# A layer with sparse attention on one core: sample compression in eighths, sample stages with loads and small operations reordered, merge started by depth

## The chip, the cores and the metric

One NeuronCore of a Trainium2 chip runs the whole program. The metric is device time in microseconds for one execution, lower is better. The profiled execution and the timed runs are different executions of the same program.

## The reference

One layer is applied to a prompt of 1024 tokens (model width 1024) and to 8 sample rows, each with 2048 past rows in paged caches. Three branches are computed: native sparse attention (attention over compressed keys, over selected blocks, and over a window, mixed by gates), a chunkwise mLSTM, and attention over a memory. Then the branches are merged and a feed-forward follows. The parts that the change touches:

```python
past_cmp = cache_kv_cmp[page_table].reshape(...)
rows_s = jnp.concatenate([past_cmp, kv_cmp_s], axis=1)
k_c, v_c, end_c = compress_kv(rows_s, cmp_pe, cmp_w1, cmp_b1, cmp_w2, k_norm_cmp)   # 127 blocks per sample
o_cmp_s, p_cmp_s = dense_attend(q_s, k_c, v_c, end_c[None, :] <= pos_s[:, None])
idx_s, valid_s = select_blocks(p_cmp_s, pos_s, -(-rows_s.shape[1] // SLC_BLOCK))     # the ranking
sel_s = gather_blocks_paged(cache_kv_slc, page_table, kv_slc_s, idx_s)
o_slc_s = slc_attend(q_rot_s, sel_s, idx_s, valid_s, pos_s)
o_win_s, win_s = win_sample(q_rot_s, kv_win_s, cache_kv_win, pos_s)
o_mem_s = mem_attend(mq_raw, cache_kv_mem, mem_q_norm)
...
yb = jnp.einsum('bsnc,ncd->bsnd', jnp.stack([o_nsa, o_ml, o_mem], axis=2), w_branch)
g = jax.nn.sigmoid(gate_raw.reshape(B, S, N_BRANCH, D_MODEL))
x = x + (g * yb).sum(2) @ w_out
```

## The kernel before

The kernel is written with explicit semaphores: each engine has its own instruction list in each block, and a block ends with a barrier of all engines, so the last engine of a block sets when the next one starts. Between the groups of stages the semaphores are cleared as well (`Stage.renew`). The stages run in this order: norm, mLSTM projections, mLSTM, sample compression (`stage_s_compress`), attention of the prompt (`stage_attention`: token projections, memory, turning, compression, and `stage_slc_win`), samples (`stage_samples`), and the tail (merge, output projection, feed-forward).

Matmuls are made exact in three passes: an operand is split into a high part (`high`, ScalarE, L160) and a low part (`low`, VectorE, L165), and `products` issues three matmuls for each pair (L177, L178, L179).

**Sample compression.** For each batch b of 8, the pages are in SBUF in a double buffer. A fill (`fill`, L2557) is 8 transposes into two PSUM banks; there are four fills for a batch, in two bank pairs in turn. Each fill is split by ScalarE (4 activations, L160) and then VectorE (4 subtractions, L165). Fill f waits until fill f-2 has been split (`x_low >= f - 1`). A batch's 96 matmuls come in four quarters of 24; a fill of the next batch stands before each quarter. The first quarter of a batch waits until all four fills of that batch are split. `project` (L2585) applies the second weight to the activated result of the batch before. At the end SyncE stores the compressed keys and values to DRAM (`kc_kept`, `vc_kept`), loads a weight of the next stage (L2536), and waits for three stores before the block's end (L2517). The second store of keys has its own semaphore `spilled`, for which ScalarE waits near the start of the token projections (L1434).

**Samples.** `stage_s_prep` loads the page table and the kept keys and values, turns the small sample rows, and waits for the loads. `stage_s_select` scores the compressed keys, takes the softmax, multiplies by the values, ranks the blocks by a 33 by 33 comparison and spreads the result; meanwhile SyncE and GpSimd issue the first loads of the next block. `stage_s_attend` goes through 24 units: window, memory and selected blocks for each batch (the last batch has the memory last). For unit u TensorE does `turn(u+1)`, `scores(u)`, `attend(u-2)`, `turn_p(u-1)`; ScalarE keeps half of the turned keys, does `softmax(u)` (L3063) and then `keep_p(u-1)` (L3074 for memory, L3076 and L3077 otherwise); VectorE keeps the other half, does `gather(u)` and `use(u-2)` (L3154, L3146). `attend(u-2)` on TensorE waits for `keep_p(u-2)` and for `use(u-3)`.

**Merge.** 72 steps of 36 matmuls: a weight tile l of 24 by a third of the tokens b. Before step 0, the first weight tile and the tokens have to be split. The first piece is four of the eight depth slices k.

## Time and profile before

| | before |
|---|---|
| median of 3 runs | 2583.96 us (2579.82 to 2584.76) |
| the profiled execution's own time | 2569.68 us |
| span of its trace | 2568.1 us |
| TensorE busy | 2389.3 us, 93% |
| VectorE busy | 1216.1 us, 47% |
| ScalarE busy | 813.6 us, 32% |
| mean granted TensorE clock | 0.965 of full speed |

The rows below are read so: a group of instructions is named by its line in the kernel, its engine and its operation, with output and input tiles. In a timeline, the first number is the start in microseconds from the span's start, the second the time until the end of the last instruction merged into the row, and the brackets hold the idle time of the engine before it and who ended it. PEclk is the granted TensorE clock as a share of 2.4 GHz, so 0.50 is 1.2 GHz.

### The profile page before, as it was taken

The numbers are of one execution on the slowest core, as the hardware profiler recorded it, in microseconds if no ns is written. First come the engines' busy times: TensorE is split into PE (matmuls) and PEld (weight loads), VectorE is DVE, ScalarE is ACT, GpSimd is POOL, SyncE is SP. The second block draws the span as 40 slices with busy tenths as digits, with TensorE's granted clock in tenths as the row PEclk, the third lists the DMA queues.
The fourth block names the chain that finished last, engine by engine and source line by source line (L and its number), as shares of the span: only waits on it lengthen the run. The fifth ranks groups of instructions, "written<-read, shape, count | busy, mean of one in ns | idle before, by whom it ended". The sixth has DMA issues, their size and how long they took to land. (4 is left out here: it accounts for less than half of the span.)

```text
span 2568.1 us, 40403 instructions
## 1 busy us (share of the span) xinstructions
PE 2389.3 (93%) x15386; PEld 2177.1 (85%) x15386; DVE 1216.1 (47%) x2160; ACT 813.6 (32%) x1779; POOL 321.0 (13%) x570
## 2 busy tenths in 40 slices
PE   6988897999877999878799999999999999999999
PEld 6977787999766889744499999987999999999997
DVE  4457665313757777466532323334434333333334
ACT  5354454444435665323321112221311111111110
POOL 1014221012204322355100000000000000000000
PEclk9998699999999999889899999999999999999999
DMA  5012432321110000277301112130211111111111
GB/s 154 21 34 67 137 109 80 98 99 34 43 35 1 1 1 1 56 183 179 98 25 50 50 42 78 50 116 1 83 50 49 34 50 50 50 39 44 50 33 66
DMA packets 216412, 156.77 MB, mean 61 GB/s; under 512 B 76338, under 2 KB 197349, under 8 KB 216164
## 3 DMA queue, kind: packets, MB, share of 16 engines
q1 hardware_dynamic: 186708, 121.96, 16.8%
q0 software_dynamic: 8160, 19.08, 2.8%
q10 hardware_dynamic: 21360, 13.22, 1.7%
q8 instruction: 123, 2.02, 0.3%
q14 instruction: 61, 0.50, 0.1%
HBM read 142.76 MB, written 15.59 MB: 62 GB/s over the span
## 5 line engine op out<-in xcount | busy, mean ns | idle before, releaser
L177 PE MATMUL ps<-brT_r,ff_wih 128*128 128x344 f32 x1008 | 322.0, 319 | 0.0
L179 PE MATMUL ps<-brT_r,ff_wi_r 128*128 128x344 f32 x1008 | 321.6, 319 | 0.0
L178 PE MATMUL ps<-xnT_r,ff_wih 128*128 128x344 f32 x1008 | 321.3, 319 | 0.0
L3765 ACT ACTIVATE ff_sa<-ps 128x344 f32<-128x344 f32 x66 | 30.3, 459 | 563.5 <-PE ps L179 563.5
L177 PE MATMUL ps<-x_r,mg_wh 128*128 128x344 f32 x576 | 185.4, 322 | 6.5 <-DVE xnT_r L165 6.5
L177 PEld LDWEIGHTS ps<-brT_r,ff_wih 128*128 128x128 f32 x1008 | 189.6, 188 | 1.0
L179 PEld LDWEIGHTS ps<-brT_r,ff_wi_r 128*128 128x128 f32 x1008 | 189.4, 188 | 0.0
L178 PEld LDWEIGHTS ps<-xnT_r,ff_wih 128*128 128x128 f32 x1008 | 189.0, 187 | 0.4
L178 PE MATMUL ps<-xnT_r,mg_wh 128*128 128x344 f32 x576 | 184.7, 321 | 0.0
L3801 DVE TENSOR_TENSOR x<-x,ps 128x512 f32<-128x512 f32 (+1 forms) x198 | 134.8, 685 | 100.9 <-PE ps L179 100.2
L179 PE MATMUL ps<-x_r,mg_w_r 128*128 128x344 f32 x552 | 176.2, 319 | 0.0
L2001 PE MATMUL ps<-a_kvsw,att_pT 128*128 128x128 f32 x1056 | 142.5, 279 | 14.9 <-ACT brT L2047 6.4
L177 PE MATMUL ps<-x_r,brT_r 128*128 128x256 f32 (+3 forms) x504 | 143.4, 285 | 7.2 <-DVE xnT_r L165 7.2
L2001 PEld LDWEIGHTS ps<-a_kvsw,att_pT 128*128 128x128 f32 x1056 | 129.2, 193 | 19.5 <-ACT att_pT L1947 11.6
L178 PE MATMUL ps<-x_r,brT_r 128*128 128x256 f32 (+3 forms) x504 | 143.0, 284 | 0.0
L179 PE MATMUL ps<-x_r,xnT_r 128*128 128x256 f32 (+3 forms) x504 | 142.8, 283 | 0.0
L3344 ACT ACTIVATE mg_sg<-ps 128x344 f32<-128x344 f32 x72 | 33.0, 458 | 319.9 <-PE ps L179 319.9
L177 PEld LDWEIGHTS ps<-x_r,mg_wh 128*128 128x128 f32 x576 | 109.3, 190 | 6.6 <-issue 6.6
L165 DVE TENSOR_TENSOR sc_xl<-ps,brT_r 64x512 fp32r<-64x512 f32 x128 | 88.2, 689 | 47.0 <-ACT brT_r L160 45.6
L178 PEld LDWEIGHTS ps<-xnT_r,mg_wh 128*128 128x128 f32 x576 | 109.1, 189 | 0.0
L2062 ACT ACTIVATE att_p<-ps,att_mx 128x640 f32<-128x640 f32 (+7 forms) x128 | 89.6, 700 | 55.7 <-DVE att_mx L2090 54.5
L3391 DVE TENSOR_TENSOR mg_tm<-mg_sg,ps 128x344 f32<-128x344 f32 x48 | 24.6, 512 | 172.0 <-ACT mg_sg L3344 172.0
(618 smaller groups left out, 5871.5 us busy)
## 6 DMA issues: line engine op xcount, KB each, us to landing
ff_wi<-in_w_ffn_in SPq DMA_DIRECT2D x42, 512.0 KB, 5.2
mg_w<-in_w_in SPq DMA_DIRECT2D x23, 512.0 KB, 4.2
ff_wo<-in_w_ffn_out SPq DMA_DIRECT2D x11, 1024.0 KB, 4.9
s_pages<-in_cache_kv_slc POOLq DMA_DIRECT2D x128, 64.0 KB, 2.8
s_pages<-in_cache_kv_slc SPq DMA_DIRECT2D x128, 64.0 KB, 2.8
sc_X<-in_cache_kv_cmp SPq DMA_DIRECT2D x56, 128.0 KB
sc_X<-in_cache_kv_cmp POOLq DMA_DIRECT2D x56, 128.0 KB, 2.4
mg_w<-in_w_branch SPq DMA_DIRECT2D x23, 256.0 KB, 4.6
```

The source lines that it names most:

```text
L165: return nc.vector.tensor_tensor(lo, x, hi.bitcast(F32), ALU.subtract)
L177: nc.tensor.matmul(out, wh, xh, start=(first and k == 0), stop=False)
L178: nc.tensor.matmul(out, wh, xl, start=False, stop=False)
L179: ins = nc.tensor.matmul(out, wl, xh, start=False, stop=(last and k == n - 1))
L2001: ins = nc.tensor.matmul(ps[:, 6 + u % 2, 0:P], pT[:, u % 2, b * P:(b + 1) * P], kv, start=(b == 0), stop=(b == hi - lo - 1))
L2062: nc.scalar.activation(p_[:, u % 2, 0:n], src, ACT.Exp, scale=-1.0, bias=mx[:, u % 4:u % 4 + 1], accum_out=sm[:, u % 4:u % 4 + 1]).then_in ...
L3344: nc.scalar.activation(sg[:, s % 2, :], ps[:, s % 4, 0:BLK], ACT.Sigmoid).then_inc(gated, 1)
L3391: chain.link(dve, nc.vector.tensor_tensor(tm, sg[:, s % 2, :], ps[:, 4 + s % 4, 0:BLK], ALU.mult))
L3765: nc.scalar.activation(sa[:, s % 2, :], ps[:, s % 2, 0:BLK], ACT.Silu).then_inc(silued, 1)
L3801: nc.vector.tensor_tensor(dst, dst, ps[0:m, 4 + i % 4, :], ALU.add).then_inc(added, 1)
```

## The change

Six places are edited:

1. Sample compression: a batch's products are issued in eighths of 12 matmuls in place of quarters of 24. The four fills stand before eighths 0, 1, 3 and 4; `project` stands after eighth 3. ScalarE's first activation of the batch and VectorE's `out` stand after the fourth split in place of the third. SyncE's last store of values is moved ahead of the weight load.
2. The kept keys and values are loaded in `stage_slc_win`, after the last query has been turned, into a part of `x2`; `stage_s_prep` no longer loads or waits for them. The page table's wait goes to SyncE and GpSimd in front of the page loads of `stage_s_select`.
3. In `stage_s_select` the multiplication by the gate (L2834) is moved behind the ranking.
4. In `stage_s_attend` ScalarE's `keep_p(u-1)` is moved ahead of `softmax(u)`.
5. At the end of `stage_s_attend` eight copies become four of twice the size.
6. Merge: the first weight tile is split in pieces of depth (0:1), (1:4), (4:12), and the first third of the tokens in (0:1), (1:2), (2:3), (3:4), (4:8); step 0 waits for each slice by itself.

```diff
@@ stage_slc_win
+        last_q = max(m for m, x in enumerate(items) if x[0] == "q")
+            @block.sync
+            def _(sp):
+                sp.wait_ge(pturned, last_q + 1)
+                for dst, name in zip(kept_rows(M), ("kc_kept", "vc_kept")):
+                    sp.dma_start(dst, M[name]).then_inc(M["kept_in"], 16)
+def kept_rows(M):
+    flat = M["x2"][:, :, :].rearrange("p t d -> p (t d)")
+    return flat[0:HD, 0:B * G * NCS], flat[:, 2048:2048 + B * G * HD]
@@ stage_s_prep
-                sp.dma_start(A["pt"][:, :], I["page_table"].rearrange("b n -> (b n)").unsqueeze(0)).then_inc(loaded, 16)
-                sp.dma_start(A["kcT"].rearrange("p n q -> p (n q)"), M["kc_kept"]).then_inc(loaded, 16)
-                sp.dma_start(A["vc"][:, :, :, :].rearrange("p b g d -> p (b g d)"), M["vc_kept"]).then_inc(loaded, 16)
-                sp.wait_ge(loaded, 48)
+                sp.dma_start(A["pt"][:, :], I["page_table"].rearrange("b n -> (b n)").unsqueeze(0)).then_inc(A["pt_in"], 16)
@@ stage_s_compress, SyncE
-                sp.wait_ge(hid, 2 * B)
-                sp.dma_start(tok_weights(M, 1, "raw"), tok_group(M, 1)).then_inc(M["tok_in1"], 16)
                 sp.wait_ge(okept, B)
                 sp.dma_start(M["vc_kept"][:, VE:], vc[:, :, :, :].rearrange("p b g d -> p (b g d)")[:, VE:]
                              ).then_inc(stored, 16)
+                sp.wait_ge(hid, 2 * B)
+                sp.dma_start(tok_weights(M, 1, "raw"), tok_group(M, 1)).then_inc(M["tok_in1"], 16)
@@ stage_s_compress, TensorE
                 for b in range(B):
-                    for k in range(4):
-                        if b + 1 < B:
-                            fill((b + 1) * NF + k)
-                        quarter(b, k)
-                        if k == 1 and b >= 1:
+                    for e in range(8):
+                        if b + 1 < B and e in (0, 1, 3, 4):
+                            fill((b + 1) * NF + (0, 1, 3, 4).index(e))
+                        eighth(b, e // 2, e % 2)
+                        if e == 3 and b >= 1:
                             project(b - 1)
@@ stage_s_compress, ScalarE and VectorE
-                        if k == 2:
+                        if k == 3:
                             gelu(b, 0)
-                        if k == 2 and b >= 1:
+                        if k == 3 and b >= 1:
                             out(b - 1)
@@ stage_s_select
+                sp.wait_ge(A["pt_in"], 16)
                 load_kinds(sp, M["I"]["cache_kv_slc"], A["pages"], A["pt"], 0, 0, A["in_k"][0], A["in_v"][0])
...
+                pe.wait_ge(M["kept_in"], 32)
...
-                dve.wait_ge(attended, 1)
-                nc.vector.tensor_tensor(oacc[:, :, :], ps[0:H, 4:6, :]..., bc(gT[:, 0, :], 2, P), ALU.mult)
                 dve.wait_ge(attended, 2)
...
                 nc.vector.tensor_scalar(imp[:, :], cnt[:, :], 15.5, -BIG, ALU.is_ge, ALU.mult).then_inc(ranked, 1)
+                nc.vector.tensor_tensor(oacc[:, :, :], ps[0:H, 4:6, :]..., bc(gT[:, 0, :], 2, P), ALU.mult)
                 dve.wait_ge(spread, 1)
@@ stage_s_attend, ScalarE
-                    softmax(u)
                     if u >= 1:
                         keep_p(u - 1)
+                    softmax(u)
@@ stage_s_attend, VectorE
-                for h in range(H):
-                    lo, g = (h % 2) * HD, h // HPG
-                    nc.vector.tensor_copy(brT[lo:lo + HD, h // 2, S:T], src)
+                for g in range(G):
+                    for q in range(2):
+                        nc.vector.tensor_copy(brT[q * HD:(q + 1) * HD, 2 * g:2 * g + 2, S:T], rows[:, 2 * g:2 * g + 2, q, :])
@@ stage_merge
+    W_FIRST = ((0, 1), (1, 4), (4, 12))
+    X_FIRST = ((0, 1), (1, 2), (2, 3), (3, 4), (4, 8))
+                    if s == 0:
+                        for k in range(4):
+                            pe.wait_ge(w_low, 1 if k == 0 else 2)
+                            pe.wait_ge(x_low, k + 1)
+                            products(nc, ps[:, 0, 0:BLK], terms[k:k + 1], first=(k == 0), last=False)
```

## Rows read from the trace of the kernel before

**Rows 1.** Tail stretch: PE, PEld, DVE, ACT, POOL busy, clock, DMA share, GB/s.
```profile
1289.00:2568.00 1279.00, 1271.63 (x7357) 1189.86 (x7355) 467.74 (x628) 229.12 (x321) 5.57 (x11) 1.00 0.17 51
```

**Rows 2.** Waits, 280 to 440 us: total, times, longest.
```profile
PE ps L177 <- DVE sc_xl L165: 11.9, 7, 2.4
```

**Rows 3.** Timeline, sample compression, 395 to 421 us: start, duration, what, idle before.
```profile
396.42 1.03 PE L2557 MATMUL ps<-cst,sc_X 128*128 128x128 f32 x8
...
397.21 0.36 PE L177 MATMUL ps<-brT_r,x_r 128*128 128x256 f32 x1
...
397.49 2.41 ACT L160 ACTIVATE brT_r<-ps 64x512 fp32r<-64x512 f32 x4 [0.78 <-PE ps L2557]
...
399.93 2.79 DVE L165 TENSOR_TENSOR sc_xl<-ps,brT_r 64x512 fp32r<-64x512 f32 x4 [0.37 <-ACT brT_r L160]
...
400.20 1.04 PE L2557 MATMUL ps<-cst,sc_X 128*128 128x128 f32 x8
...
420.54 0.38 PE L177 MATMUL ps<-brT_r,x_r 128*128 128x256 f32 x1 [2.39 <-DVE sc_xl L165]
```

**Rows 4.** Timeline, end of compression and start of the next stage.
```profile
442.51 0.50 SPq L2541 DMA_DIRECT2D kc_kept<-brT  x1
...
447.01 7.22 ACT L160 ACTIVATE brT_r<-xnT 128x512 fp32r<-128x512 f32 x7 [10.68 <-PEq L102]
```

**Rows 5.** DMA issues, 430 to 447 us: count, KB, us to landing.
```profile
kc_kept<-brT SPq DMA_DIRECT2D x1, 127.0 KB, 3.5
```

**Rows 6.** SyncE's waits over the whole span: total, times, longest.
```profile
SPq L2380 <- DMA s_vc<-vc_kept: 4.7, 1, 4.7
...
SPq L2517 <- DMA vc_kept<-sc_vc: 2.6, 1, 2.6
```

**Rows 7.** Timeline, sample preparation and selection.
```profile
1071.19 0.16 DVE L2419 COPY s_gT<-ps 8x24 f32<-8x24 f32 x1
...
1075.54 5.02 SPq L2771 DMA_DIRECT2D s_vrow<-memT  x8
...
1088.83 1.21 DVE L2834 TENSOR_TENSOR s_oacc<-ps,s_gT 8x1024 f32<-8x1024 f32 x1 [3.14 <-PE ps L2801]
...
1098.17 0.42 DVE L2851 COPY s_selneg<-ps 8x264 f32<-8x264 f32 x1 [1.14 <-PE ps L2809]
...
1101.00 0.94 PE L3032 MATMUL ps<-s_knT,s_qz 128*8 128x1 f32 x32 [2.87 <-PEq L2764]
```

**Rows 8.** SyncE's 16 page issues in the selection: first and last start.
```profile
L2440 SPq DMA_DIRECT2D s_pages<-in_cache_kv_slc x16: 542/543/1119, 1088.1 to 1099.8; - x16
```

**Rows 9.** Waits, 1101 to 1277 us.
```profile
PE ps L3021 <- ACT sa_pT L3074: 14.1, 7, 2.1
```

**Rows 10.** Timeline, sample attention: one batch, and two later starts of L3021.
```profile
1138.46 2.00 ACT L3063 ACTIVATE sa_s<-sa_s,sa_mx 8x2049 f32<-8x2049 f32 x1 [6.44 <-DVE sa_mx L3131]
...
1138.71 0.34 DVE L3154 SCALAR_TENSOR_TENSOR s_oacc<-ps,sa_sm,s_oacc 8x128 f32<-8x128 f32 x1
...
1140.66 1.88 PE L3021 MATMUL ps<-x,sa_pT 128*4 128x512 f32 x4 [2.13 <-ACT sa_pT L3074]
...
1223.58 2.43 PE L3021 MATMUL ps<-x,sa_pT 128*4 128x512 f32 x4 [2.14 <-ACT sa_pT L3074]
...
1247.40 1.02 PE L3021 MATMUL ps<-s_rows,sa_pT 128*4 128x512 f32 x2 [1.26 <-ACT sa_pT L3074]
```

**Rows 11.** Two short stretches, columns as in rows 1.
```profile
1226.00:1228.00 2.00, 2.00 (x19) 1.96 (x19) 1.77 (x2) 0.12 (x1) 1.56 (x3) 0.50 0.68 144
...
1286.00:1288.00 2.00, 2.00 (x14) 2.00 (x13) 2.00 (x3) 2.00 (x3) 0.00 (x0) 0.95 0.00 0
```

**Rows 12.** Timeline, end of the sample attention and first matmul of the merge.
```profile
1274.14 1.41 DVE L3178 COPY brT<-ps 64x8 f32<-64x8 f32 x8 [1.84 <-PE ps L3051]
...
1278.90 1.59 DVE L165 TENSOR_TENSOR xnT_r<-xnT,x_r 128x1376 fp32r<-128x1376 f32 x1 [0.55 <-ACT x_r L160]
...
1280.64 0.62 PE L177 MATMUL ps<-x_r,mg_wh 128*128 128x344 f32 x1 [6.54 <-DVE xnT_r L165]
```

More of the change, by code:

```diff
@@ L2377, in stage_s_prep @@
         sem = st.sem
-        turned, kept, loaded = (sem(n) for n in ("turned", "kept", "loaded"))
+        turned, kept = (sem(n) for n in ("turned", "kept"))
         chain = Chain(sem("step"))
@@ L2559, in fill, with eighth @@
                     ins.then_inc(turned, 1)
-                def quarter(b, k):
-                    cc = k // 2
-                    if k == 0:
+                def eighth(b, k, part_):
+                    cc, lo = k // 2, k % 2 * 8 + 4 * part_
+                    if k == 0 and part_ == 0:
                         pe.wait_ge(x_low, NF * (b + 1))
-                    if k % 2 == 0 and b >= 1:
+                    if lo == 0 and b >= 1:
                         pe.wait_ge(activated, 2 * (b - 1) + cc + 1)
-                    if k % 2 == 0 and b == 0:
+                    if lo == 0 and b == 0:
                         pe.wait_ge(w_low, cc + 1)
@@ L2572, in quarter @@
                                    [((w1h[:, cc, r, :], w1l[:, cc, r, :]), (part(xh, r), part(xl, r)))
-                                    for r in range(k % 2 * 8, k % 2 * 8 + 8)], first=(k % 2 == 0), last=(k % 2 == 1))
-                    if k % 2:
+                                    for r in range(lo, lo + 4)], first=(lo == 0), last=(lo == 12))
+                    if lo == 12:
                         ins.then_inc(hid, 1)
@@ L3194, in stage_samples @@
         A["rows0"] = st.sb("rows", [P, 2, 2048])[:, :, :]
+        A["pt_in"] = st.sem("pt_in")
         for n in ("in_win", "in_mem"):
@@ L3294, in _ @@
                     n, j = loads[l]
-                    if b == 0:
-                        pe.wait_ge(w_low, l + 2 if l else 1)
-                    if l == 0:
-                        pe.wait_ge(x_low, 2 * b + 1)
+                    if b == 0 and l:
+                        pe.wait_ge(w_low, l + 3)
+                    if l == 0 and b:
+                        pe.wait_ge(x_low, x_count(b) + 1)
                     if s >= 4:
@@ L3330, in _ @@
                 act.wait_ge(M["mg_in"][0], 16)
[L3331 removed]
+                split_first(slice(*W_FIRST[0]))
                 for b in range(NB3):
[L3333 to L3335 removed]
+                    for lo_, hi_ in x_pieces(b):
+                        high(nc, xh[:, lo_:hi_, tok(b)], xnT[:, lo_:hi_, tok(b)]).then_inc(x_high, 1)
+                        if b == 0 and lo_ == 0:
+                            split_first(slice(*W_FIRST[1]))
+                        if b == 0 and lo_ == 3:
                             act.wait_ge(M["mg_in"][1], 16)
[L3337 removed]
+                            split_first(slice(*W_FIRST[2]))
                     split_b(0, b)
```

46 lines of the change are left out of this document (24 added, 22 removed).

## The prediction

> **What bounds the kernel now.** I read the stretches by stage first, then TensorE's waits in each, then the timeline around each wait, then SyncE's own waits. From 1289 us to the end TensorE is busy 1271.63 of 1279 us at full clock [rows 1]: the feed-forward and most of the merge hold nothing to win, and whatever is saved ahead of them moves them as a block. Ahead of them TensorE is the engine that sets the pace inside the stages, and stage boundaries are set by whoever arrives last. The reader should see four places where TensorE or a boundary waits: seven waits of 11.9 us in all in the sample compression [rows 2], two DMA waits of SyncE at block ends, 2.6 and 4.7 us [rows 6], seven waits of 14.1 us in the sample attention [rows 9], and the 6.5 us before the merge's first matmul [rows 12].
>
> **Compression in eighths.** A fill takes TensorE 397.21 - 396.42 = 0.79 us; a fill and a quarter take 400.20 - 396.42 = 3.78, so an eighth is (3.78 - 0.79) / 2 = 1.5. ScalarE begins 1.07 after the fill's start and takes 2.41, VectorE follows with 2.79: a fill is split some 6.3 us after it began [rows 3]. Between the last fill of a batch and the next batch's first quarter TensorE has only 0.79 + 3.0 + 0.79 of work, so it waits: 2.39 in the last case, where no fill stands between [rows 3], and (11.9 - 2.39) / 6 = 1.58 in the six others [rows 2]. After the change, from a batch's start at 0: fill 0 ends at 0.8, eighth 0 at 2.3, fill 1 at 3.1, eighths 1 and 2 at 6.1. Fill 2 needs fill 0 split, at 6.3 to 6.4: a new wait of about 0.25. It ends at 7.15, eighth 3 at 8.65, `project` at 9.5. Fill 3 needs fill 1 split. ScalarE took fill 1 behind the first activation, at 4.0, so VectorE ends it at 9.2: no wait. Fill 3 begins at 9.5, its ScalarE part at 10.6, its VectorE part at 13.05 and ends at 15.85, and the four eighths run to 16.35. The next batch's first eighth then finds its data ready, also in the last batch. The old waits go (11.9), seven new ones of 0.25 and 0.03 of slack in each come (2.0): a gain of 9.9 us. Bounds: 11.9 if the new wait is nothing; 6 if each of the seven is 0.8, that is, if the splits behind the closer pair of fills end half a microsecond late. ScalarE's activation moved behind the fourth split is wanted only by the next batch's first eighth, 2.8 us later. The page loads wait for fills that now come earlier, so they are not late.
>
> **The store moved ahead of the weight load.** SyncE waits 2.6 us for the small store of values at the stage's end [rows 6]. Moved ahead, it lands before SyncE gets there, and the block can end 2.6 earlier. But something is late next: the next stage's ScalarE first waits for the last store of keys (`spilled`), issued at 442.51 and landing after 3.5, at 446.0 [rows 4, 5]; ScalarE's first instruction there starts at 447.01 [rows 4]. That store is not moved. So only 447.0 - 446.05 = 0.95 is gained. SyncE's weight load is one issue later and is wanted much later. Bounds 0.3 (the load now sits directly ahead of the keys in the queue) and 2.6.
>
> **Kept keys and values loaded in the attention.** SyncE is idle there and nothing is queued behind its wait for the last query. In the preparation SyncE waits 4.7 [rows 6] while VectorE ends at 1071.35 and the next block starts at 1075.54 [rows 7]. Without the two loads VectorE is last; with the 0.45 us that a block's end took after SyncE's wait, the next block starts at 1071.8: gain 3.75. The page table is waited for later, behind 8 + 4 + 1 issues on SyncE and the 2.4 us of GpSimd's mask, 2.5 us or more after its issue at 1068.9. Bounds 3.2 and 4.2.
>
> **The gate behind the ranking.** VectorE's chain loses 1.21 us at 1088.83 [rows 7] and gets the operation back under TensorE's spreading, where VectorE waits 1.14 anyway [rows 7]. But VectorE ends at 1098.59, and TensorE's next block starts at 1101.00 [rows 7]. Who is last is SyncE: its sixteenth page issue starts at 1099.8 and takes 0.54 [rows 8], ending at 1100.3. That queue is neither shortened nor moved against the block's start. So I cost this at 0. Bounds -0.1 and 1.1.
>
> **Probabilities kept first.** The memory unit's `keep_p` stands behind the 2.00 us softmax of the selected blocks on ScalarE, though its input is ready: TensorE is through at 1138.53 and attends at 1140.66, after 2.13 idle [rows 10]. Ahead of the softmax, `keep_p` is done near 1136.6. Then `attend` waits for VectorE's `use` of the window unit, which ends at 1138.71 + 0.34 = 1139.05 [rows 10]. This is the late thing next: TensorE starts at 1139.1 and not 1138.5, keeping 0.6 of idle in six batches, so 14.1 - 3.6 = 10.5 is gained. The softmax of the selected blocks isn't delayed, as `keep_p` is over by then. The other pairs: the window's softmax now waits for the turned probabilities of the selected unit, some 1 us later than now, and the memory's for those of the window unit, 3 us later; both are wanted by TensorE over 4 us after that. Bounds 3 (the softmax's end, 1140.55 [rows 10], governs the following turn, and everything else with it) and 12.5.
>
> **The clock.** In the sixth of these batches the granted clock is 0.50 (1.2 GHz) at 1226 to 1228 us [rows 11], right after one such idle time. From 1140.66 to 1223.58 four batches take 20.73 each; the next interval is 23.82 [rows 10], so 3.1 us more. With idle times a third as long I expect no such fall: gain 3.1, bounds 0 and 3.1.
>
> **Copies at the end.** Eight copies take 1.41 [rows 12], 0.18 each; four of twice the elements (16 for 64 partitions) at 0.18 give 0.7: gain 0.7, bounds 0.3 and 0.9.
>
> **Merge by depth.** VectorE's subtraction on four slices takes 1.59 and ends at 1280.49, 3.5 us after the block's start; TensorE follows at 1280.64 [rows 12]. By depth the first piece is a quarter: TensorE can start about 1.3 after the block's start, 2.35 earlier. It then does a slice each 0.86 at the half clock and ends the fourth at 4.9. The second half of the tokens is split no earlier than now (6.2 after the start, since VectorE's total is the same), so TensorE pauses 1.3. The clock rose near 1286.1, so 5.4 us after the first matmul [rows 11, 12]; if it rises as long after the new start, the rest runs at the full clock, and step 0 ends at 10.1 in place of 11.9 after the block's start. I take 1.3. Bounds 1.9, and -1.1 if the pause puts the rise off by its own start over again. TensorE, from 1289 us on, never waits, so this passes to the end.
>
> [...]
>
> **The sum.** 9.9 + 0.95 + 3.75 + 0 + 10.5 + 3.1 + 0.7 + 1.3 = 30.2 us. The profiled execution took 2569.68, which becomes 2539.5. The median of the timed runs is 14.3 higher; I take the same gain from it: 2583.96 - 30.2 = 2553.8, say 2554.
>
> **Rivals.** (a) The fills collide: closer fills wait for VectorE each time and the compression gains 4 instead of 9.9, time 2560. For it: two of four fills now follow an eighth after another. Against: VectorE and ScalarE both have idle time in each batch [rows 3]. Chance 0.10. (b) Another wait takes the place in the attention: `turn_p` waits for the softmax or `attend` for `use`, and with the clock term it gains 4 instead of 13.6, time 2563.5. For it: VectorE's 1139.05 and ScalarE's 1140.55 [rows 10] stand close ahead of the old times. Against: TensorE's own 1.88 of `attend` fills that stretch. Chance 0.12. [...] Chance 0.2, inside the range. (d) Slower: in the sample attention, 176 us long, the granted clock stays at 1.2 GHz. By the timeline the half clock lasted some 7 us and cost 3.1, so 0.45 a microsecond; the gain of 27.1 outside the clock term is gone when it lasts over 60 us, and the kernel is slower by 0.2% from 72. At 90 us the time is 2583.96 - 27.1 + 40.5 = 2597. Against: idle times get shorter. Chance 0.03. (e) The moved loads don't do what they should, because the preparation is held by something else as long: time 2557.5. Chance 0.05, inside the range too.
>
> **The numbers.** My forecast 0.7 (with (c) and (e) as variants of it), (a) 0.10, (b) 0.12, (a) and (b) together 0.03, (d) 0.03, rest 0.02. The lower end takes the good bounds of compression, store and attention (2, 1.6, 2) and a little for the runs' scatter: 2545. The upper one takes in (a) and (b) singly: 2566. Under 0.2%, 5.2 us, a measurement of this kernel can hardly tell from no change; faster by more than that 0.95, the same 0.02, slower 0.03.
>
> **What would show it.** Compression: no wait before L177 in batches 1 to 7, small waits of 0.25 before L2557; intervals between batches of 16.3 in place of 17.7. Boundary: no DMA wait at SyncE's L2517, and ScalarE's first instruction about 1 us earlier against the last key store. Preparation: the block after it 0.45 us behind VectorE's last copy. Selection: 25.4 us long as before, SyncE last. Attention: waits of TensorE for L3074 gone, about 0.6 for L3154 in their place, interval 19.2 in place of 20.7, clock 1.00. Merge: first matmul 1.3 after the block's start, a pause of 1.3 in step 0. It is wrong if new waits before L2557 sum to over 6 us, if intervals in the attention stay above 20, or if the clock drops where it didn't before.

## The result, and the profile after

Four timed executions of the kernel before, the three of the table ahead of the prediction among them, have a median of 2581.89 us (2577.26 to 2584.76); four of the changed kernel have 2543.01 (2541.01 to 2544.89). The ratio is 0.9856, 95% interval 0.9835 to 0.9877: 38.9 us, 1.5%, faster. The forecast was 2554 us with a range from 2545 to 2566: the sign is right, the gain was larger than forecast, and the time lies 2.0 us below the range. The profiled execution took 2543.22 (span 2541.6), 26.5 less than the profiled one of before (2569.68), and that is less than the 30.2 that I summed. So the steps have to be read one by one, and two questions stay for the runs: which terms were wrong, and why the timed gain is 12 us more than that between the two profiles.

The stage's waits in the compression (290 to 440 us; total, times, longest), to be held against [rows 2]:

```profile
PE ps L2569 <- DMA sc_X<-in_cache_kv_cmp: 3.8, 1, 3.8
PE ps L2569 <- DVE sc_xl L165: 2.3, 7, 1.1
```

The wait of L177 for `sc_xl` is gone, and the fills (L2569) wait instead. Of the seven waits in the last row, the longest (1.05 us, at 289.76) stands in the kernel before as well, ahead of the first batch; the new ones are six of 0.17 to 0.23 us, 1.2 us in all, where the prediction counted seven of 0.28. The timeline of one batch shows one of them, in the middle of the batch:

```profile
329.82 1.04 PE L2569 MATMUL ps<-cst,sc_X 128*128 128x128 f32 x8
...
332.13 1.04 PE L2569 MATMUL ps<-cst,sc_X 128*128 128x128 f32 x8
...
336.24 1.09 PE L2569 MATMUL ps<-cst,sc_X 128*128 128x128 f32 x8 [0.17 <-DVE sc_xl L165]
...
346.19 1.03 PE L2569 MATMUL ps<-cst,sc_X 128*128 128x128 f32 x8
```

A batch is 346.19 - 329.82 = 16.37 us long; forecast 16.35. Now the end of the stage, and the preparation with the selection, which answer to [rows 4, 7]:

```profile
433.28 0.51 SPq L2553 DMA_DIRECT2D kc_kept<-brT  x1
...
437.18 3.38 ACT L160 ACTIVATE brT_r<-xnT 128x512 fp32r<-128x512 f32 x3 [10.09 <-DMA kc_kept<-brT]
...
1063.18 0.16 DVE L2431 COPY s_gT<-ps 8x24 f32<-8x24 f32 x1
...
1063.82 5.04 SPq L2785 DMA_DIRECT2D s_vrow<-memT  x8
...
1084.63 1.20 DVE L2863 TENSOR_TENSOR s_oacc<-ps,s_gT 8x1024 f32<-8x1024 f32 x1
1085.84 0.42 DVE L2867 COPY s_selneg<-ps 8x264 f32<-8x264 f32 x1
...
1089.49 0.94 PE L3048 MATMUL ps<-s_knT,s_qz 128*8 128x1 f32 x32 [3.69 <-PEq L2778]
```

ScalarE's first instruction behind the compression names the last store of keys as what released it, as forecast; the block itself started at 435.73, so the values' store no longer holds it. From the issue of that store to ScalarE's first instruction it is 3.90 us in place of 4.50, which is 0.6 gained where 0.95 was forecast: the store took 3.9 us to land and not 3.5. The block behind the preparation starts 0.48 us behind VectorE's last copy (1063.34 to 1063.82): the 4.7 us of [rows 6] are gone. In the selection VectorE is done at 1086.26 and the next block begins at 1089.45. SyncE's page issues there (count, then duration in ns, then first and last start) end last, at 1088.2 + 0.54, as in [rows 8]:

```profile
L2452 SPq DMA_DIRECT2D s_pages<-in_cache_kv_slc x16: 542/543/1337, 1076.4 to 1088.2; - x16
```

The sample attention and the merge stand against [rows 9, 10, 11, 12]: first the waits from 1105 to 1252 us, then the timeline, then two stretches with the granted clock in the third column from the end.

```profile
PE ps L3037 <- DVE s_oacc L3171: 4.4, 7, 0.7
...
PE ps L3037 <- ACT sa_pT L3093: 0.5, 1, 0.5
```

```profile
1108.17 1.88 PE L3037 MATMUL ps<-s_rows,sa_pT 128*4 128x512 f32 x4 [0.67 <-DVE s_oacc L3171]
...
1127.43 1.02 PE L3037 MATMUL ps<-x,sa_pT 128*4 128x512 f32 x2 [0.67 <-DVE s_oacc L3171]
...
1249.95 0.73 DVE L3195 COPY brT<-ps 64x16 f32<-64x16 f32 x4 [1.25 <-PE ps L3067]
...
1253.49 0.62 PE L177 MATMUL ps<-x_r,mg_wh 128*128 128x344 f32 x1 [3.58 <-DVE xnT_r L165]
...
1258.21 0.43 PE L177 MATMUL ps<-x_r,mg_wh 128*128 128x344 f32 x1 [1.06 <-DVE xnT_r L165]
```

```profile
1110.00:1250.00 140.00, 133.20 (x880) 73.25 (x879) 90.09 (x188) 43.55 (x103) 67.26 (x94) 1.00 0.67 162
...
1262.00:2541.00 1279.00, 1272.55 (x7358) 1190.88 (x7356) 469.98 (x629) 231.53 (x323) 5.57 (x11) 1.00 0.17 51
```

The forecast signs are there: waits of 0.67 us for `use` in place of 2.13 for `keep_p`, batches 19.26 us apart (forecast 19.2), the clock 1.00 from 1110 to 1250 us, four copies in 0.73, TensorE's first matmul 1.42 us behind the merge block's start (1252.07), a pause of 1.06, and from there to the end a TensorE as busy as in [rows 1]. The waits moved as forecast. What was wrong is the size of terms and the time that they were taken from, and it took repeats of the kernel before to see which.

### The profile page after: what moved, and what is told of

Read it like the earlier page. It is cut to its first block and busy times, and to the rows that moved or that the text cites. A ratio compares the mean times of both kernels' runs of the same rounds, so it can differ in the third digit from the quotient of the medians.

```text
span 2541.6 us, 40409 instructions
## 1 busy us (share of the span) xinstructions
PE 2392.3 (94%) x15386; PEld 2180.1 (86%) x15386; DVE 1216.2 (48%) x2160; ACT 813.7 (32%) x1783; POOL 321.1 (13%) x570
## 5 line engine op out<-in xcount | busy, mean ns | idle before, releaser
L177 PE MATMUL ps<-brT_r,ff_wih 128*128 128x344 f32 x1008 | 322.0, 319 | 0.0
L177 PEld LDWEIGHTS ps<-brT_r,ff_wih 128*128 128x128 f32 x1008 | 189.6, 188 | 1.0
L177 PE MATMUL ps<-x_r,mg_wh 128*128 128x344 f32 x576 | 185.1, 321 | 4.6 <-DVE xnT_r L165 4.6
L177 PE MATMUL ps<-x_r,brT_r 128*128 128x256 f32 (+3 forms) x504 | 143.6, 285 | 6.6 <-DVE xnT_r L165 6.6
L177 PEld LDWEIGHTS ps<-x_r,mg_wh 128*128 128x128 f32 x576 | 108.8, 189 | 5.1 <-DVE memT_r L165 3.6
```

The costliest lines, as they stand in the source:

```text
L177: nc.tensor.matmul(out, wh, xh, start=(first and k == 0), stop=False)
```

## The experiments

Each kernel was timed beside the kernel before on the same chip; the comparisons below ran on four chips, on which the kernel before has medians of 2575.4 to 2577.8 us. "By part" below means the length of a stretch between the same two matmuls of two traces. A "fall" is a stretch in which the granted clock is 0.50 between stretches at 1.00; a "full" one costs 3.08 us, a "short" one 1.6.

**The kernel before, again.** No edit.

> The kernel before, unchanged, profiled and timed once more. Its three timed executions took 2579.8 to 2584.8 us, its profiled one 2569.7, while the changed kernel's profiled execution (2543.2) lies among its timed ones (2541.0 to 2544.9). Theory 1: the profiled execution of before was an untypically quick one; this one should take 2578 to 2585, and its timeline of granted clocks should show where the 12 us lie: more half-clock stretches right behind waits in the sample attention (up to six falls of some 3 us each in place of one) or in the sample compression. Theory 2: profiled executions of this kernel are simply quicker than timed ones: again 2570 profiled beside 2580 timed, with the same single fall of the clock. Ratio to the kernel before 1.000 within 0.002 in both.

Twelve executions have a median of 2577.64 us (2570.20 to 2581.57), and the twenty-four that they were compared with 2576.8 (2566.5 to 2583.3); the profiled one took 2578.6. The trace shows the fall of the clock behind TensorE's wait for `keep_p` not once but twice (first stretches, with the clock in the third column from the end; then the matmuls behind the waits):

```profile
1211.00:1216.00 5.00, 5.00 (x33) 4.85 (x33) 2.46 (x3) 1.24 (x4) 3.27 (x5) 0.50 0.81 201
1235.00:1240.00 5.00, 5.00 (x33) 4.90 (x33) 2.93 (x4) 1.04 (x3) 2.88 (x4) 0.50 0.84 218
```

```profile
1188.01 1.88 PE L3021 MATMUL ps<-x,sa_pT 128*4 128x512 f32 x4 [2.14 <-ACT sa_pT L3074]
...
1208.74 2.43 PE L3021 MATMUL ps<-s_rows,sa_pT 128*4 128x512 f32 x4 [2.14 <-ACT sa_pT L3074]
...
1232.56 2.35 PE L3021 MATMUL ps<-x,sa_pT 128*4 128x512 f32 x4 [2.14 <-ACT sa_pT L3074]
```

The waits are as long as ever, 2.14. From 1188.01 to 1208.74 it is 20.73, from 1208.74 to 1232.56 it is 23.82: the half clock costs 3.08 us, and it can be told by the matmuls' own 2.43 in place of 1.88. A shorter stretch at 0.50, behind the first of the waits (1124.20), costs 1.6 more. Theory 1 holds in kind (more falls), with two and not six. Of the 9.0 us between the two profiles of the same kernel these are 4.7; the rest is scatter elsewhere, by part 2.4 before the compression, 0.4 at its end, 0.5 in the attention of the prompt and 1.2 ahead of the first wait of the sample attention. Over the executions the time goes with the mean granted clock: 0.967 at 2567.3 us, 0.959 at 2583.3.

**Probabilities kept first, alone.**

```diff
-                    softmax(u)
                     if u >= 1:
                         keep_p(u - 1)
+                    softmax(u)
```

> The kernel before with one edit: in the sample attention ScalarE keeps the probabilities of the previous unit ahead of the softmax. The prediction gave this 10.5 us of waits and 3.1 of clock, 13.6 in all. Theory 1 (the timed executions of before lose a further 12 us in falls of the clock behind these very waits): 22 to 27 us faster in the timed medians, and the granted clock is 1.00 over the stage. Rival (the further 12 us lie in a part that this edit doesn't touch): 10.5 to 14 us faster. Other rival (no effect beyond the moved wait): under 5.

2560.19 us against 2576.8: ratio 0.9941 (0.9928 to 0.9954), 16.6 us. That is between the two expectations, 10.5 to 14 and 22 to 27. The waits and the clock over the stage:

```profile
PE ps L3021 <- DVE s_oacc L3155: 4.4, 7, 0.7
```

```profile
1120.00:1260.00 140.00, 134.48 (x869) 72.50 (x867) 91.24 (x194) 46.01 (x105) 68.91 (x96) 1.00 0.67 165
```

The waits are those of the changed kernel, and there is no fall. By part, the waits give 10.2 us; the falls give 3.08 against the trace that stands ahead of the prediction, and 7.8 against a trace of before with two full falls and the short one. The 16.6 lie between these sums. Six executions lie within 5.7 us and twenty-four of before within 16.8, which suggests that the edit takes much of the scatter with it, though six are few.

**Eighths, alone.** The hunks for TensorE, ScalarE and VectorE in the compression, without the moved store.

```diff
...
-                    for k in range(4):
...
+                    for e in range(8):
+                        if b + 1 < B and e in (0, 1, 3, 4):
+                            fill((b + 1) * NF + (0, 1, 3, 4).index(e))
+                        eighth(b, e // 2, e % 2)
...
```

> The kernel before with the compression alone changed: fills amid eighths. The prediction gave 9.9 us (bounds 6 to 11.9); the changed kernel's trace shows batches of 16.24 us in place of 17.7 and 11.4 us in all between first fill and the turning of the keys. If the further 12 us of the timed medians come from waits of this stage that let the clock fall in timed executions, the gain is 18 to 24; if not, 9 to 12.

2563.88 against 2576.8, ratio 0.9958 (0.9938 to 0.9977): 12.9 us. The stage's trace shows batches of 16.2 to 16.4 us, and from the stage's third fill (284.56 in the trace of before, the first behind a wait for a split) to the first turned key 135.86 us in place of 148.3. That is 12.4, above my upper bound of 11.9. The waits explain 10.7 of it (the old 11.9 less the new 1.2). Where the rest comes from is in the trace of before, in rows that the prediction didn't use: the starts of the first fill in two batches that follow each other, and a stretch of 2 us:

```profile
309.97 1.04 PE L2557 MATMUL ps<-cst,sc_X 128*128 128x128 f32 x8
...
329.46 0.71 PE L2557 MATMUL ps<-cst,sc_X 128*128 128x128 f32 x5
```

```profile
314.00:316.00 2.00, 2.00 (x12) 2.00 (x11) 1.96 (x4) 0.01 (x1) 0.54 (x1) 0.50 0.59 175
```

That batch lasted 19.49 us and the later ones 17.6 to 17.8: here too a fall of the clock, 1.8 us dear. Six of seven traces with the old compression have it, and none of the eleven with the eighths. But in the seventh of the old ones (merge alone, below) the half clock at the stage's start lasted longer instead, and the stage took 148.17 us all the same. Nine of the eleven with the eighths start in this way too; they take 136.5 to 137.4 us, and only this trace and that of the last experiment below, without the longer start, 135.9. So the fall is gone for certain, and its 1.8 us in part.

**Merge by depth, alone.** The merge's hunks.

```diff
...
+                        for k in range(4):
+                            pe.wait_ge(w_low, 1 if k == 0 else 2)
+                            pe.wait_ge(x_low, k + 1)
+                            products(nc, ps[:, 0, 0:BLK], terms[k:k + 1], first=(k == 0), last=False)
...
```

> The kernel before with the merge's first splits by depth alone. The prediction gave 1.3 us (bounds -1.1 to 1.9); the changed kernel's trace shows step 0 ending 10.02 us after the block's start in place of 11.94, with the clock up 3.3 us after the first matmul. Expected: 1.3 to 1.9 us faster in the medians, which five rounds can hardly tell from nothing; in its trace a pause of 1.0 to 1.3 in step 0 and its end 10.0 to 10.2 after the block's start. Rival: the pause puts off the clock's rise, step 0 ends 13 after the block's start and the kernel is 1 us slower.

2573.77 against 2576.8, ratio 0.9993 (0.9975 to 1.0011): the interval holds no change, and twelve executions can't tell 1.3 us. In the trace the first matmul comes 2.3 us earlier and step 0 ends 0.53 earlier, counted from the transposes of the outputs:

```profile
1287.80 0.62 PE L177 MATMUL ps<-x_r,mg_wh 128*128 128x344 f32 x1 [4.28 <-DVE xnT_r L165]
...
1292.52 0.65 PE L177 MATMUL ps<-x_r,mg_wh 128*128 128x344 f32 x1 [0.91 <-DVE xnT_r L165]
```

```profile
1288.00:1294.00 6.00, 5.09 (x17) 4.54 (x18) 5.75 (x8) 6.00 (x7) 0.00 (x0) 0.50 0.93 248
1296.00:1298.00 2.00, 2.00 (x14) 2.00 (x14) 2.00 (x2) 2.00 (x2) 0.00 (x0) 1.00 0.03 8
```

The clock rises between 1294 and 1296 us, 6 to 8 after the first matmul (before: 5.4 to 5.7). Counted from the first of those transposes (1281.85), the rise is where it was: 13.7 to 13.9 us behind it in four traces of before, and 14.0 here. TensorE starts 2.3 us earlier, but the full clock doesn't come earlier with it. From the transposes to the end of step 0 it takes 16.5 us in all four traces of before and 16.02 here. In the changed kernel's first trace it is 13.33, with the clock back after 8.1, and in its second (below) 15.68, with the clock back after 14.4. Of ten traces of that kernel and its variants two are like the first and eight like the second (15.3 to 15.7).

**Loads moved, alone.** The kept keys and values (`kept_rows`) are loaded by SyncE in the attention, and the page table is waited for later.

```diff
...
-                sp.dma_start(A["kcT"].rearrange("p n q -> p (n q)"), M["kc_kept"]).then_inc(loaded, 16)
...
-                sp.wait_ge(loaded, 48)
...
+                for dst, name in zip(kept_rows(M), ("kc_kept", "vc_kept")):
+                    sp.dma_start(dst, M[name]).then_inc(M["kept_in"], 16)
...
```

> The kernel before with one edit: the kept keys and values loaded by SyncE in the attention stage, the page table waited for later. Forecast by the prediction: 3.75 us (bounds 3.2 and 4.2), and no other effect: in the trace the preparation's block lasts 2.9 us in place of 6.6 and the selection 25.4 to 25.7 as before. Rival: the loads' landing or SyncE's wait for the last query delays something in the attention stage, and the gain is under 2. Falls of the clock are left as they were, so the timed executions scatter over 15 us as those of before and the median tells the term only roughly.

2573.09 against 2577.84, ratio 0.9983 (0.9967 to 0.9999): 4.7 us in the medians, with a wide interval, as expected. The trace has the preparation at 1070.61 to 1073.51, 2.90 us in place of 6.61, and the selection about as long as before (25.6 us beside 25.4):

```profile
1070.61 0.27 SPq L2398 DMA_DIRECT2D s_pt<-in_page_table  x1
...
1073.51 5.04 SPq L2783 DMA_DIRECT2D s_vrow<-memT  x8
...
1099.17 0.94 PE L3047 MATMUL ps<-s_knT,s_qz 128*8 128x1 f32 x32 [2.65 <-PEq L2776]
```

So the preparation gives 3.7 us, the forecast's 3.75.

**The changed kernel, again.** No edit.

> The changed kernel once more, so that it stands beside many executions of the kernel before on one chip. If the gain beyond my 30.2 us came from falls of the clock in ordinary executions of before (two or three in the sample attention at 3.08 us each, where its first profiled execution had one), the gain is 33 to 37 us and the executions of before scatter over 15 us, those of the changed kernel over 5. If my sum was right and the first comparison a matter of few runs, 28 to 32.

2544.73 (2542.13 to 2546.64) against 2576.86: ratio 0.9871 (0.9855 to 0.9888), 32.1 us. That falls just short of the first expectation (33 to 37) and just over the second (28 to 32), so this run alone decides neither. Over all runs of this study 73 executions of before have a median of 2577.1 (2566.5 to 2585.9) and eight of the changed kernel 2543.7 (2541.0 to 2546.6): 33.4 us. Only twelve of the 73 took 2579.8 us or more, and the three behind the table ahead of the prediction are among the twelve.

**The gate put back.** VectorE's multiplication ahead of the ranking again, first in the changed kernel, then in one where SyncE is not last.

```diff
...
+                dve.wait_ge(attended, 1)
+                nc.vector.tensor_tensor(oacc[:, :, :], ...)
                 dve.wait_ge(attended, 2)
...
```

> The changed kernel with the gate's multiplication put back ahead of the ranking. Forecast by the prediction: no difference (bounds -0.1 and 1.1 us), because SyncE's sixteenth page issue ends after VectorE does; ratio to before as that of the changed kernel within 0.0005. In the trace VectorE ends its ranking 1.2 us later (some 1.4 us before SyncE's last issue ends), and the selection stage is as long as before the undoing, 25.6 us. Rival: the operation counts in full, and the stage is 1.2 us longer.

2543.27 us, ratio 0.9867 (0.9851 to 0.9884); with the gate moved it was 0.9871 (0.9855 to 0.9888). VectorE now ends at 1089.04 and SyncE's last issue at 1090.3, so SyncE is last still; the selection takes 1065.63 to 1091.01, 25.4 us, and 25.6 with the gate moved. Moving it is worth nothing here, as forecast.

**Rows of new values loaded by ScalarE.**

```diff
             def _(sp):
...
-                    sp.dma_start(A["vrow"][q:q + 1, b % 2, :, :], kv[b:b + 1, :, 1, :]).then_inc(vrows, 16)
...
-                sp.wait_ge(vrows, 16 * B)
...
             def _(act):
...
+                    act.dma_start(A["vrow"][q:q + 1, b % 2, :, :], kv[b:b + 1, :, 1, :]).then_inc(vrows, 16)
                 act.wait_ge(maxed, 1)
...
```

> The changed kernel with the eight loads of the new values' rows, 5.04 us of issues at the head of SyncE's queue in the selection stage, issued by ScalarE, which is idle there. By the reading that SyncE's issues end that stage, they end 5 us earlier, VectorE (1086.3) becomes the last, and the next stage's block starts some 2.4 us earlier: the stage lasts 23.2 in place of 25.6, the kernel 2.4 us less than the changed kernel. Rival: the stage's end hangs on something else (a landing, GpSimd), and it stays at 25.6.

The selection stage takes 1063.16 to 1086.09, 22.9 us. Now VectorE is the last, and SyncE's sixteenth page issue started 2.2 us before VectorE's last copy:

```profile
1082.93 0.54 SPq L2452 DMA_DIRECT2D s_pages<-in_cache_kv_slc  x1
...
1085.17 0.42 DVE L2866 COPY s_selneg<-ps 8x264 f32<-8x264 f32 x1
1086.09 2.06 ACTq L2460 DMA_DIRECT2D x<-in_cache_kv_win  x4
1086.12 0.94 PE L3047 MATMUL ps<-s_knT,s_qz 128*8 128x1 f32 x32 [0.98 <-PEq L2778]
```

2.7 us of the stage are gained. The median is 2542.37 us, 2.4 below the changed kernel's on the same chip; the ratio to before is 0.9867 (0.9851 to 0.9884), so the intervals overlap and the trace carries the finding. This and the next are the quickest versions of the study.

The same kernel with the gate's multiplication back ahead of the ranking:

> As the run before it, and the gate's multiplication back ahead of the ranking. With SyncE's queue out of the way the 1.2 us of the multiplication should now count in full: the selection stage lasts 24.4 in place of 23.2. If it still lasts 23.2, moving the gate is worth nothing even there, and another engine sets that stage's end.

Here the gate counts: the stage takes 1062.63 to 1086.58, 23.95, 1.0 us more than with the gate moved. The median, 2541.88, can't tell 1 us. An edit that is worth nothing beside SyncE's queue is worth 1 us once that queue is short.

**The old order put back in the changed kernel,** twice.

```diff
+                    softmax(u)
                     if u >= 1:
                         keep_p(u - 1)
-                    softmax(u)
```

> The changed kernel with one edit undone: in the sample attention ScalarE does the softmax ahead of keeping the probabilities again. If the waits bring the falls of the clock, they come back here: six waits of 2.1 us, intervals of 20.73 between batches, and two or three of them 3.08 longer with the granted clock at 0.50 in them; 16 to 18 us slower than the changed kernel in the medians, with a scatter over 10 us and more. If the falls of before came from something else that the change took away elsewhere, intervals of 20.73 without longer ones, and 10 to 11 us slower.

2557.03 us (2555.0 to 2563.6), ratio to before 0.9930 (0.9907 to 0.9953). That is 12.3 above the changed kernel, which ran on another chip, and the profiled execution has no fall between the batches: the six waits are back (with a seventh of 1.25 us, 14.1 in all, 2.1 the longest) at a clock of 1.00.

```profile
PE ps L3037 <- ACT sa_pT L3090: 14.1, 7, 2.1
```

```profile
1110.00:1255.00 145.00, 130.93 (x854) 71.35 (x855) 89.47 (x187) 45.38 (x105) 69.02 (x96) 1.00 0.63 159
```

That misses the first expectation (16 to 18) and is near the second (10 to 11, without falls), and it forbids the simple reading that a wait of 2.1 us brings the fall. Whether the changed kernel's other edits kept the falls away was open; so it was run again, with two further profiles of before.

> The changed kernel with the old order of softmax and kept probabilities, a second profile. The first had the six waits of 2.1 us and no fall between batches. If the falls are drawn anew, a number from 0 to 3, and 2555 to 2564 us; if the changed kernel's other edits prevent them, none again.

> The kernel before, unchanged, one more profile. Five profiles with the old order in the sample attention on top of the kernel before showed 1 to 3 full falls of the clock between its batches (6.8 us at half clock, 3.08 us late each), a sixth one, on top of the changed kernel, none. If the number is drawn anew at each execution, this one shows 1 to 3 again and takes 2570 to 2583, more with more falls; if a kernel's first profile is the rule, one fall and 2570.

> The kernel before, unchanged, yet one more profile; as the run before it. Two different numbers of falls in equal kernels on one chip would show that the trace of one execution can't size the clock term.

The same kernel, a second time, has one fall (2555.5 us):

```profile
1192.00:1198.00 6.00, 6.00 (x36) 5.12 (x36) 3.09 (x4) 1.64 (x4) 3.04 (x5) 0.53 0.88 257
```

The kernel before took 2573.49 and 2578.47, with two falls each, at different places: behind the matmuls at 1182.87 and 1206.68 in the third profile,

```profile
1182.87 2.36 PE L3021 MATMUL ps<-x,sa_pT 128*4 128x512 f32 x4 [2.13 <-ACT sa_pT L3074]
...
1206.68 2.29 PE L3021 MATMUL ps<-s_rows,sa_pT 128*4 128x512 f32 x4 [2.13 <-ACT sa_pT L3074]
...
1230.49 1.88 PE L3021 MATMUL ps<-x,sa_pT 128*4 128x512 f32 x4 [2.13 <-ACT sa_pT L3074]
```

and in the fourth at the places of the second, with the shorter one again. So the number of falls and their places differ between executions of one kernel. Seven profiles with the old order on top of the kernel before have 1, 2, 2, 2, 3, 2 and 2 falls of 3.08 us, and five of them a short one of 1.6; the two with it on top of the changed kernel have 0 and 1, at the same waits of 2.13 us.

**Waits twice as long.** The old order, and two copies into unused memory between softmax and `keep_p`.

```diff
                     softmax(u)
+                    if units[u][0] == "slc" and u >= 1:
+                        act.wait_ge(exped, u + 1)
+                        nc.scalar.activation(spare[0], s_[0:H, u % 2, 0:1024], ACT.Copy)
+                        nc.scalar.activation(spare[1], s_[0:H, u % 2, 1024:2048], ACT.Copy)
```

> The same, and in each batch ScalarE makes two further copies of 1024 scores (about 1.1 us each, into unused memory) between the softmax of the selected blocks and keeping the probabilities, so that TensorE's six waits are some 4.3 us in place of 2.1. The waits alone cost 13 us more than with the old order: 2570. If longer waits bring the fall more surely, up to six of them: intervals of 23 + 3 us, the clock at 0.50 in each, and a time near 2588. If the number of falls has nothing to do with the waits' length, 2570 to 2577.

2599.05 us (2595.9 to 2604.7), ratio 1.009 (1.0069 to 1.0111). The expectation was near 2588. Behind every one of the six waits of 4.4 us, and behind the seventh of 3.55, the clock is at 0.50, for some 3 us behind the first and for some 10 at the others, where a full fall of before lasted some 7. Two of the waits, and one of the stretches:

```profile
1134.81 3.57 PE L3038 MATMUL ps<-x,sa_pT 128*4 128x512 f32 x4 [4.41 <-ACT sa_pT L3091]
...
1162.11 3.58 PE L3038 MATMUL ps<-s_rows,sa_pT 128*4 128x512 f32 x4 [4.42 <-ACT sa_pT L3091]
```

```profile
1136.00:1142.00 6.00, 6.00 (x29) 3.78 (x28) 2.46 (x3) 0.33 (x2) 1.74 (x3) 0.50 1.05 174
```

Batches are 27.3 us apart in place of 20.73. Of the 6.6 more, the longer wait makes 2.3 and the clock 4.3, not the 3 that was expected. So waits do bring the falls, and length makes them sure: at 4.4 us six of six, at 2.1 us one to four of six in the profiles on top of before (short falls counted) and none or one on top of the changed kernel, at 0.67 us none in six profiles of the new order. The Trainium skill, "TensorE: Matmul & The Clock Gate", section "HAM oscillation — how this bites in real kernels", describes matmul bursts that are separated by waits and start each time at the lowered clock. This run agrees: the half clock came back at every wait. In that page's kernel, as it adds up its time, the clock costs about a third of what the waits do (26.7 us beside 76.4); here it costs 4.3 us a batch beside a wait of 4.4.

**The window unit's weighting earlier.** An attempt at the 0.67 us that are left: VectorE does `use` of the window unit ahead of the maximum over 2049 scores.

```diff
...
+                    if early(u):
+                        use(u - 2)
                     dve.wait_ge(skept, chunk0[u + 1])
                     chain.link(dve, nc.vector.tensor_reduce(mx[0:nh, ...], ...))
...
```

> The changed kernel with VectorE's weighting of the window unit's output moved ahead of the maximum of the selected blocks' scores. TensorE's wait of 0.67 us for it, six times, should go: intervals of 18.6 in place of 19.26, 4.0 us in all less what comes late next. VectorE's maximum starts later, by its wait for the window's products, about 1 us, and so do the softmax and everything that TensorE turns after it. If that has slack, 3 to 4 us faster; if not, the wait moves to the turning of the selected blocks' probabilities and the gain is 0 or a loss of up to 3.

2551.14 us, ratio to before 0.9899 (0.9878 to 0.9920), where the changed kernel had 0.9871 and 2544.73 on another chip: some 6 us slower than it. By part the sample attention takes 167.0 us in place of 159.3 and 158.7 in two traces of the changed kernel, so the loss is in this stage. The wait moved, as the second expectation says, but it costs more than its length:

```profile
1131.11 1.15 PE L3011 MATMUL ps<-cst,sa_s 8*128 8x8 f32 x16 [1.07 <-ACT sa_s L3079]
...
1152.32 1.15 PE L3011 MATMUL ps<-cst,sa_s 8*128 8x8 f32 x16 [1.08 <-ACT sa_s L3079]
1171.89 1.15 PE L3011 MATMUL ps<-cst,sa_s 8*128 8x8 f32 x16 [1.07 <-ACT sa_s L3079]
```

```profile
1133.00:1135.00 2.00, 2.00 (x11) 2.00 (x10) 0.83 (x3) 0.95 (x3) 2.00 (x4) 0.50 0.97 206
```

The softmax of the selected blocks now starts later, TensorE waits 1.07 us for it in six batches in place of 0.67 for `use`, and four of the six waits are followed by a short fall: 1131.11 to 1152.32 is 21.21 us, the next interval, without one, 19.57. Four falls of 1.6 us are most of the loss.

The same edit together with the rows loaded by ScalarE:

> The changed kernel with both: the rows of new values loaded by ScalarE (its stage measured 22.9 us in place of 25.6), and the window unit's weighting moved ahead of the maximum. If the second gains 3 to 4, both give 5.5 to 6.5 us over the changed kernel, 2537 to 2539 us; if the second gains nothing, 2.5.

2547.75 us (2544.1 to 2554.0). The second edit gained nothing, so the expectation of 2537 to 2539 fell with it, and the 2.5 us over the changed kernel did not come either; by part the sample attention takes 166.0 us, 7.2 more than with the rows by ScalarE alone. The trace has three short falls. Two stand behind waits of 1.08 us; the third stands behind a wait of 0.54:

```profile
1238.65 5.33 PE L3036 MATMUL ps<-s_pages,sa_pT 128*8 128x128 f32 x32 [0.54 <-ACT sa_pT L3092]
```

```profile
1240.00:1242.00 2.00, 2.00 (x12) 1.26 (x10) 0.00 (x0) 0.00 (x0) 0.00 (x0) 0.50 0.00 0
```

From there to the next wait it is 6.2 us, where it is 4.55 in the traces without this fall. All traces have this wait. The only other one with a fall at it is that of the waits of 4.4 us, where a wait of 2.0 ended 3 us earlier. So a wait isn't safe by being short alone.

## Why the prediction was off

The table has the lengths of the stretches in us, between the same matmuls, in three traces: the one of before that stands ahead of the prediction, the fourth profile of before (span 2576.9 us; the execution took 2578.5, 1.4 over the median of 73), and the changed kernel's first. They add up to the spans.

| stretch | before | before, fourth | after | gain on the fourth | forecast |
|---|---|---|---|---|---|
| up to the compression's third fill | 284.56 | 286.59 | 286.74 | -0.2 | 0 |
| to the first turned key | 148.46 | 148.30 | 137.06 | 11.2 | 9.9 |
| to the next stage's first matmul | 15.39 | 15.10 | 14.79 | 0.3 | 0.95 |
| attention, to 1060 us | 611.58 | 612.95 | 613.39 | -0.4 | 0 |
| preparation and selection | 41.01 | 41.03 | 37.51 | 3.5 | 3.75 |
| sample attention | 171.36 | 177.20 | 159.27 | 17.9 | 13.6 |
| outputs turned, copies, step 0 of the merge | 16.55 | 16.55 | 13.33 | 3.2 | 2.0 |
| rest | 1279.19 | 1279.18 | 1279.51 | -0.3 | 0 |
| sum | 2568.1 | 2576.9 | 2541.6 | 35.3 | 30.2 |

- **The first step that failed is "The clock"**, as the prediction put it: "gain 3.1, bounds 0 and 3.1". The mechanism was right: with shorter waits there was no fall between these batches. The size was not. It was read off one execution that had one fall, and its upper bound was that same execution. Seven profiles have two full falls on the mean, 2.0 x 3.08 + 5/7 x 1.6 = 7.3 us. One more fall, 1.8 us, stood in the compression in the same trace, and no term was given to it. In the six traces with both old orders these falls come to 4.9 to 10.8 us, 8.7 on the mean, where the term was 3.1.
- **The second step that failed is the baseline**, and it is the larger part of the miss. "The median of the timed runs is 14.3 higher; I take the same gain from it": a profile 14 us under three timed executions, in a kernel whose clock falls behind waits, is a sign that its executions scatter by something that the change touches. Those three gave 2583.96, and 73 give 2577.1. Of the 10.8 us between forecast and result, 6.9 are this, 3.2 that the gain is 33.4 and not 30.2, and 0.7 that the first four executions of the changed kernel have a lower median than all eight. Why the first three took so long is not known; chance is possible (twelve of 73 are as slow), and a difference of the chip that they ran on was not ruled out. The lower end of the range added nothing for the clock either.
- **Compression**: the mechanism was right, and a batch came true to 0.1 us. The new waits are 1.2 us and not 2.0. The upper bound of 11.9 bounded the waits and so left out what the waits do to the clock. In the changed kernel's trace 1.2 of the 12.4 is given back (137.06 us beside 135.86) at the stage's start, which ran longer at the half clock: from the third fill to the fill that opens the second batch it takes 26.84 us, beside 25.68 with the eighths alone.
- **Store**: right in kind; the keys' store is last. The stretch is 15.0 to 16.75 us long in eight traces with the old order of the stores (15.4 on the mean) and 14.1 to 14.8 in ten with the new one (14.3), 1.1 beside the forecast's 0.95. This edit wasn't run alone.
- **Loads**: 3.7 against 3.75. **Gate**: 0 against 0, and the reason is shown by taking eight issues out of SyncE's queue.
- **Probabilities first**: 10.2 of waits against 10.5, and the late thing next is `use`, with 0.67 against 0.6. Rival (b), another wait in the same place, did not come.
- **Copies**: 0.68 against 0.7. **Merge**: 1.3 was forecast. In the first trace it is 16.55 - 13.33 - 0.7 = 2.5, in the second only 16.55 - 15.68 - 0.7 = 0.2, alone 0.5. The forecast took the clock to rise as long after TensorE's new start as after the old one. In eight of ten traces it rose 13.7 to 14.5 us behind the transposes, as in the kernel before, and so 8.5 to 9.6 us after the first matmul in place of 5.4 to 5.7. That eats the gain and doesn't turn it into the loss of 1.1 that the lower bound allowed for. Whether the pause is what holds the clock back was not tested: no run starts TensorE earlier without a pause. Here the forecast was too high, and the first profile flattered it.
- Rivals (a), (d) and (e) did not come. For (d), an attention at the half clock with shorter waits, no trace gives any sign.

What stays open: what decides, at waits of equal length, whether the clock falls. Equal kernels gave one fall and two, none and one; the two kernels with the earlier weighting had a short fall behind four and behind two of six equal waits, and the second one more behind a wait of 0.54 us. That the position of the wait in time matters would fit this, but it is not shown. Nor is it explained why the old order brought fewer falls on top of the changed kernel (0 and 1) than on top of before (1 to 3); two profiles are few.

## What to carry to other kernels

A wait of TensorE between dense stretches is not worth its own length only: here 14 us of waits took 7 more by the clock, and waits in another stage up to 1.8. So list every stretch at the half clock that follows a wait, in every stage, and put the term's upper bound at one fall behind every such wait. When the profiled execution and the timed ones differ by a large part of the gain that is argued about, take more executions of the kernel before, forecast the difference of two typical ones, and suspect the scatter itself to be part of the gain. And before an edit at a stage's end is costed, ask which engine's queue is last: the same 1.2 us operation was worth nothing beside SyncE's 16 issues and 1.0 without eight others ahead of them.

## What was not expected of the hardware

- Waits of 1.07 us brought short falls of the clock (1.6 us each, behind four of six in one profile and two of six in another), waits of 0.67 none in six profiles, a wait of 0.54 one in a single profile, and waits of 4.4 us one each time. Waits 0.4 us longer went with a kernel that is some 6 us slower.
- Starting the merge's matmuls 2.3 us earlier did not bring the full clock earlier: in eight of ten traces it came 13.7 to 14.5 us behind the transposes ahead of them, beside 13.7 to 13.9 in four traces of the kernel before.
- The same kernel took from 2566.5 to 2585.9 us over 73 executions, a spread of 0.75%, and its mean granted clock went from 0.967 to 0.958 with it; six executions with the new order alone lay within 5.7 us.
- SyncE spends 4.9 us (1071.54 to 1076.44) between its last row load and its first page issue of the selection, in which its queue issues no transfer; the trace has eight reads of a page number (L2446) there, some 0.55 us apart. Nothing was tried on it; with the rows on ScalarE's queue VectorE is last, so in that version it is no longer in the stage's way.
